# Sample attention of a hybrid decoder step: keys loaded by head pair, turned on VectorE in blocks of 32, scores of each sequence in four strips

## The reference, cut to what matters

```python
def dilated_attention_sample(q, k_all, v_all, rel_bias):   # q: (B=8, T=4, H=8, 64)
    for (w, d) in ((128, 1), (512, 4), (2048, 16)):        # keys at distance 0, d, 2d .. w
        ...
    s = einsum('bthc,btkhc->bthk', q, kg) * 64 ** -0.5 + bias
    p = softmax(where(valid, s, NEG))                      # one softmax over all key lists
    return einsum('bthk,btkhc->bthc', p, vg)
```

## Time and profile before

| | us |
|---|---|
| median of 3 runs | 1074.83 (1074.57 to 1074.99) |
| the profiled execution | 1073.11 |
| its span, first to last instruction | 1071.3 |
| start to the convolution stage | 281.2 |
| convolution stage with sample attention | 218.5 |
| output projection and router | 164.9 |
| experts | 272.1 |
| gated tail | 134.6 |

### The profile page before, as it was taken

How to read it: one execution, slowest core, us unless ns; L and a number is a source line. 1 busy time by engine, 2 the same in 40 slices (tenths; PEclk the granted TensorE clock), 3 DMA queues, 4 the chain that set the end, 5 groups by cost and what they waited for, 6 DMA issues and landing times.

```text
span 1071.3 us, 15537 instructions
## 1 busy us (share of the span) xinstructions
PE 1025.6 (96%) x5818; PEld 615.3 (57%) x5818; DVE 528.3 (49%) x1213; ACT 295.2 (28%) x621; POOL 177.6 (17%) x191
## 2 busy tenths in 40 slices
PE   6999999899999999999999998999999988899997
PEld 5888876556778877766445554334433323345443
DVE  4836545777753544344447875341111101068674
ACT  2332322777422321201002232111111111245331
POOL 0000000123600020015301223223131211130000
PEclk9999999899999999999999999999999989999999
DMA  9724133870654454656537534999999999784321
GB/s 320 193 86 147 44 92 107 231 212 20 219 167 155 148 163 152 219 204 230 213 118 294 203 127 161 405 403 420 418 414 414 421 413 398 311 342 165 123 79 79
DMA packets 103388, 241.85 MB, mean 226 GB/s; under 512 B 20342, under 2 KB 61214, under 8 KB 88784
## 3 DMA queue, kind: packets, MB, share of 16 engines
q1 hardware_dynamic: 92672, 211.83, 54.5%
q0 software_dynamic: 9920, 26.38, 6.4%
q10 hardware_dynamic: 720, 2.62, 0.6%
HBM read 206.84 MB, written 38.67 MB: 229 GB/s over the span
## 4 chain that ended last, share of the span: by engine, by line
PE 87%; DMA 7%; DVE 3%; issue 1%; ACT 1%; SPq 1%; POOL 0%; DVEq 0%; POOLq 0%; ACTq 0%
PE pair L2988 14%; PE pair L2678 13%; PE pair L3231 11%; PE pair L3338 7%; PE pair L3253 6%; PE pair L3076 5%; PE pair L3056 5%; DMA R<-in_w_down 3%; PE pair L3333 3%; PE pair L2812 2%; PE pair L2786 2%; PE pair L2827 2%; DMA R<-in_w_up 2%; PE pair L3218 2%; PE pair L2889 1%; PE pair L2906 1%
## 5 line engine op out<-in xcount | busy, mean ns | idle before, releaser
L2988 PE MATMUL pair<-R 128*128 128x264 f32 x672 | 160.4, 389 | 0.0
L3231 PE MATMUL pair<-R 128*32 128x512 f32 (+2 forms) x896 | 150.3, 603 | 6.4 <-DMA R<-in_w_up 4.8
L2678 PE MATMUL pair<-R 128*128 128x256 f32 x672 | 150.8, 384 | 2.4 <-DVE R L1730 2.4
L2678 PEld LDWEIGHTS pair<-R 128*128 128x128 f32 x672 | 128.0, 193 | 21.2 <-DVE R L1730 3.0
L2988 PEld LDWEIGHTS pair<-R 128*128 128x128 f32 x672 | 123.5, 190 | 23.0 <-issue 4.4
L2400 DVE TENSOR_TENSOR R<-pair,R 128x256 f32<-128x256 f32 x21 | 8.9, 425 | 208.7 <-ACT R L1542 208.7
L3231 PEld LDWEIGHTS pair<-R 128*32 128x32 f32 (+2 forms) x896 | 48.8, 125 | 92.4 <-issue 88.8
L3253 PE MATMUL pair<-R,bias 128*32 128x512 f32 (+2 forms) x448 | 79.0, 621 | 4.0 <-DMA R<-in_w_down 3.5
L3338 PE MATMUL pair<-R 128*128 128x512 f32 x168 | 73.0, 593 | 0.0
L3076 PE MATMUL pair<-R 128*128 128x512 f32 x128 | 58.5, 599 | 0.0
L3338 PEld LDWEIGHTS pair<-R 128*128 128x128 f32 x168 | 31.5, 190 | 38.2 <-issue 38.0
(11 more groups left out here) (383 smaller groups left out, 1496.5 us busy)
## 6 DMA issues: line engine op xcount, KB each, us to landing
R<-in_w_gate SPq DMA_DIRECT2D x32, 1024.0 KB, 15.6
R<-in_w_up SPq DMA_DIRECT2D x32, 1024.0 KB, 19.8
R<-in_w_down SPq DMA_DIRECT2D x32, 1024.0 KB, 21.0
R<-in_cache_k SPq DMA_DIRECT2D x8, 1024.0 KB, 5.1
R<-in_cache_v SPq DMA_DIRECT2D x8, 1024.0 KB, 4.9
R<-y_dram SPq DMA_DIRECT2D x16, 512.0 KB, 4.9
R<-in_w_in SPq DMA_DIRECT2D x15, 512.0 KB, 6.8
R<-xq_dram SPq DMA_DIRECT2D x1, 7168.0 KB, 26.1
```

The costliest lines, as they stand in the source:

```text
L2678: last = mm(qbank(p, part, k), lhs[:, c, :], rhs[:, c, :], start=(c == 0), stop=(c == 3))
L2988: last = mm(cbank(u, chain), w[:, c, :], xq[:, x, c, j, :], start=(c == 0 and n in (0, 1, 3)), stop=(c == 3), skip_group_check=True)
L3231: last = mm(bk[2 + u][r, :].rearrange("p (w f) -> p w f", w=2), xgT[u][:, c, r], wgu[s][:, :, c, :], start=(c == 0), stop=(c == DC - 1))
```

## The change

Keys are loaded otherwise. Per sequence and head pair `gg` one DMA brings the near rows and three bring the far rows, 128 features of 512 bytes each, to the 32 partitions `32*gg` and up: 16 DMAs to a key item where there were 4. On each partition lie 28 blocks of 128 features, one for each 32 keys. Values come with rows in another order, four DMAs as before, near rows as 2 KB pieces, far rows with the four rows of a group as the outermost dimension of the source.

VectorE turns the keys: `dve.transpose` of a 128 x 896 view, each 32 x 32 block by itself, four times per sequence, the j-th of every fourth feature. TensorE's 224 key turns and the copies behind them are gone. The contraction of a score now runs over 32 features of all four head pairs at once, four accumulating steps to a sequence, with a query tile that is zero outside its head. The four PSUM strips hold four quarters of the keys (256 columns each; the last one 128 cached keys and 4 x 32 columns for the new ones), so each sequence has its own 128 x 256 score tile, in two banks in turn. Every strip has its own minimum and sum; the exponentials are turned (2 turns per sequence) and weigh the values unnormalised; after sequences 3 and 7 the minima and sums are turned, a factor per strip is formed on VectorE and ACT, turned back and applied when the weighed values are masked. The bias table is made in strips too. The query and key of the sample tile are turned with every fourth column.

```diff
+        def load_item(i): ...
+            if kind == "k":
+                for gg in range(NG):
+                    rows, f = slice(32 * gg, 32 * gg + 32), slice(P * gg, P * gg + P)
+                    sp.dma_start(KL[i % 3][rows, 0:16, :], src[b][PAST - NEAR:PAST, f].rearrange("(k c) f -> c k f", c=32)).then_inc(arrived, 16)
+                    for k in range(FARC):
+                        sp.dma_start(KL[i % 3][rows, 16 + 4 * k:20 + 4 * k, :],
+                                     src[b][512 * k:512 * k + 512, f].rearrange("(c a) f -> c a f", a=16)[:, 0:4, :]).then_inc(arrived, 16)
+                return
+            sp.dma_start(near_kv, src[b][PAST - NEAR:PAST, :].rearrange("(s p) d -> p s d", s=4)).then_inc(arrived, 16)
             for k in range(FARC):
-                sp.dma_start(far_kv[:, k, :], src[b][512 * k:512 * k + 512, :].rearrange("(p a) d -> p a d", a=16)[:, 0:NT, :]).then_inc(S(f"ring_in{i % 3}"), 16)
+                sp.dma_start(far_kv[:, k, :], src[b][512 * k:512 * k + 512, :].rearrange("(c a) d -> a c d", a=16)[0:4]).then_inc(arrived, 16)
...
+        def turn_keys(b, j):          # VectorE
+            if j == 0:
+                slot, arrived = item("k", b)
+                dve.wait_ge(S(f"ring_in{slot}"), arrived)
+                if b >= 1:
+                    dve.wait_ge(S("ss_done"), b)
+            dve.transpose(keysT[:, j, :].rearrange("p (b n) -> p b n", n=32),
+                          KL[item("k", b)[0]][:, :, j:P:4]).then_inc(S("kt_done"), 1)
+
+        def score_sample(b): ...
+            dve.tensor_tensor_reduce(Es[b % 2], bk[6 + b % 2][:, 0:ROW], bias_s, -1.0, 3e38, ALU.add, ALU.min,
+                                     nms[:, b:b + 1]).then_inc(S("ss_scored"), 1)
...
         for u in range(UNITS):        # VectorE
...
             join_first(u)
-            if u >= 1:
-                sample_part(*SAMPLE_PARTS[k])
-            second_keys(*SAMPLE_PARTS[k])
+            if u == 1:
+                score_sample(0)
+            if 1 <= u < NB:
+                turn_keys(u, 0)
+                turn_keys(u, 1)
...
+            if 1 <= u < NB:
+                turn_keys(u, 2)
+                turn_keys(u, 3)
...
             join_lower(u)
...
             lower_out(u)
...
+            if 1 <= u < NB:
+                score_sample(u)
...
+            if u == 0:
+                spread_q(1)
             if u == 1:
+                spread_q(2)
...
+        def score_keys(b):            # TensorE
+            pe.wait_ge(S("kt_done"), 4 * b + 4)
...
+            for j in range(4):
+                start, stop = j == 0, j == 3
                 for k in range(FARC):
+                    mm(out[strips[k], 0:ROW].rearrange("p (h n) -> p h n", h=2), query(b)[:, j, :], keys_of[j][k], start=start, stop=stop)
+                mm(out[strips[3], 0:P], query(b)[:, j, :], keysT[:, j, FARC * P:NEAR], start=start, stop=False)
+                last = mm(out[strips[3], P:ROW].rearrange("p (a n) -> p a n", n=SAMP), query(b)[:, j, :],
+                          kts[:, j, :].unsqueeze(1).broadcast_to([P, 4, SAMP]), start=False, stop=stop)
...
             for n in range(PRODUCTS): # TensorE
                 conv_product(u, n)
...
+                if n == 1:
+                    if u == 1:
+                        score_keys(0)
+                    if 2 <= u <= NB:
+                        turn_ps(u - 1)
...
+                    if 5 <= u <= 9:
+                        sum_values(u - 5)
+                    if u >= 9:
+                        weigh_values(u - 4)
+                if n == 3 and u == 1:
+                    turn_ps(0)
+                if n == 3 and 4 <= u <= 8:
+                    weigh_values(u - 4)
+                if n == 5:
+                    if 1 <= u < NB:
+                        score_keys(u)
```

More of the change, by code:

```diff
@@ L64 @@
 SK = NEAR + FAR
-SKN = SK + SAMP
+ROW = 2 * P
+KEYS = SK
+KB = KEYS // 32
 CAP = 128
@@ L181 @@
 ITEMS = [("k", b) for b in range(5)] + [("v", 0), ("k", 5), ("v", 1), ("k", 6), ("v", 2), ("k", 7)] + [("v", b) for b in range(3, NB)]
+ISSUES = {"k": NG * (1 + FARC), "v": 1 + FARC}
 def item(kind, b):
     i = ITEMS.index((kind, b))
[L187 to L200, removed]
+    return i % 3, sum(16 * ISSUES[k] for k, _ in ITEMS[i % 3:i + 1:3])
+RING_USED = tuple(sum(16 * ISSUES[k] for k, _ in ITEMS[s::3]) for s in range(3))
 NSTAT = 6
@@ L480, in _build, with query @@
     PTf = view(R1, 20928, 2, 6, P)
[L482 to L486, removed]
+    keysT = view(R1, 14784, 4, KEYS)
+    keys_of = [[R1[:, 14784 + KEYS * j:14784 + KEYS * j + 1024].rearrange("p (h n) -> p h n", h=2)[:, :, P * k:P * k + P]
+                for k in range(FARC)] for j in range(4)]
+    Es = [view(R1, 18368 + ROW * k, ROW) for k in range(2)]
+    sx_min, sx_sum = (R1[0:4, 18880 + 32 * k:18912 + 32 * k] for k in range(2))
+    sx_d, sx_w = (R1[0:4, 18944 + P * k:18944 + P * k + P] for k in range(2))
+    PTs = view(R1, 19296, 4, 2, P)
+    qb = [view(bias, 512, 4, 4, 32), view(R1, 22368, 2, 4, 32), view(lg_all, 0, 2, 4, 32)]
+    def query(b):
+        return qb[0][:, b] if b < 4 else qb[b // 2 - 1][:, b % 2]
     sel = view(R1, 22624, NT)
+    head = misc[:, 3 * NE + 13:3 * NE + 15]
     as_raw = view(gqk, 0, CC, SAMP)
@@ L1435, in sample_part, with exp_sample @@
[L1435 to L1445 removed]
+        def exp_sample(b):
+            act.wait_ge(S("ss_scored"), b + 1)
+            act.activation(Es[b % 2], Es[b % 2], ACT.Exp, bias=nms[:, b:b + 1], scale=-1.0,
+                           accum_out=dens[:, b:b + 1]).then_inc(S("ss_exp"), 1)
@@ L2096, in normalise_sample, with spread_q @@
-        def normalise_sample(g):
-            dve.wait_ge(S("ss_exp"), g + 1)
-            then(dve.reciprocal(rdens, dens))
-            dve.tensor_scalar(Es, Es, rdens, None, ALU.mult).then_inc(S("ps_ready"), 1)
+        def spread_q(k):
+            first, n = ((0, 4), (4, 2), (6, 2))[k]
+            tok = slice(NT * first, NT * (first + n))
+            for gg in range(NG):
+                rows = slice(32 * gg, 32 * gg + 32)
+                for hh in range(2):
+                    dve.tensor_scalar(qb[k][rows, :, :, 8 * gg + hh:8 * gg + 8:2], qts[rows, :, tok].rearrange("p j (b t) -> p b j t", t=NT),
+                                      head[rows, hh:hh + 1], None, ALU.mult).then_inc(S("qbd"), 1)
@@ L2897, in score_keys @@
-        def score_keys(b):
-            g, bb = divmod(b, 4)
-            pe.wait_ge(S("kn_free"), 4 * b + 4)
-            pe.wait_ge(S("kf_free"), 4 * b + 4)
-            pe.wait_ge(S("qbd"), 8 * g + 8)
-            if bb == 0:
-                pe.wait_ge(S("ss_scored"), g) if g else pe.wait_ge(S("ot_free"), NGROUP)
-            for c0, c1, rhs in ((0, NEAR, near), (NEAR, SK, far), (SK, SKN, kts)):
-                for gg in range(NG):
-                    last = mm(bank[3][strips[gg], c0:c1], qbd[bb][:, gg, :], rhs[:, gg, :],
-                              start=(bb == 0 and c1 <= SK), stop=(bb == 3 and c1 != SK))
-            last.then_inc(S("ss_done"), 1)
@@ L2941, in sum_values @@
+            mm(bk[3][strips[3], :], PTs[:, b % 4, 1, 96:128], V[:, PT, :], start=False, stop=True).then_inc(S("so_full"), 1)
         def sum_values(b):
```

350 lines of the change are left out of this document (150 added, 200 removed).

## The result

The changed kernel took 1088.56 us (median of 4 runs, 1086.93 to 1090.78) against 1074.91 for the kernel before, timed beside it: ratio 1.0111, 95% interval 1.0085 to 1.0138. The forecast was 1060.8, faster. The profiled execution has a span of 1087.1 us where before had 1071.3.

The account below looks back on a forecast made before the run. TensorE was taken to bound the convolution stage: 194.1 us without waits plus 11.1 lost gives 205.2, 13.3 less; with the bias table 14.05 less, so 1059.1 profiled and 1060.8 median, range 1056 to 1064.

Parts of the forecast that it names:

- TensorE's work: Convolution stage without waits: 218.5 less 25.3 of key turns and 1.3 of wait, plus 1.4 scores and 0.8 turns, 194.1 us.
- The turn: VectorE's four 128 x 896 key turns per sequence: 1.09 us each, 4.3 per sequence, hidden from units 2 and 3 on.
- The keys' rate: Key loads at the stage's start: 512-byte pieces at 267 GB/s, 3.9 us per MB, SP's issue at 0.64 us slower.
- rival A: SP issues at 0.46 us per DMA, so weights land at 309 before they are wanted; 1051.9 us, chance 25%.
- the 11.1: Losses in first units: 1.0, 0.5, 4.3 for weights, 0.8, 1.2, 2.2 for turns and 1.1 for clock, 11.1 us.
- the forecast hole: Start of unit 2: TensorE stands still 3 to 6 us, ending when the weights land; a sign the forecast is right.
- The sum's term for the clock: First units, TensorE working about half the time: one clock fall of 3.4 us, 2.3 under the turns' wait, 1.1 counted.
- From unit 3 on the ring is ahead by 2 to 12 us: Loads from unit 3 on: data come 2 to 12 us ahead of need, so no loss was counted there.
- the 205.2 of the forecast: Whole convolution stage: 194.1 without waits plus 11.1 of losses, 205.2 us, 13.3 less than before.
- rival B: Values' far rows on four of sixteen DMA engines in units 4 to 7: about 4 us lost, 1064.8 us, chance 20%.
- Outside the stage: Later stages: order of events fixed relative to the convolution stage's end, so an earlier stage moves them as a whole.
- C: Keys into 32 partitions at half of 267 GB/s, 21 to 24 us lost, about 1073 us, no change; chance 10%.

Follow-up runs that it names:

- e7: Changed kernel with far values loaded with 32 as outermost dimension and weights of units 2 and 3 issued behind the first key item; 1061.19 us.
- e2: Changed kernel with VectorE turning 32 neighbouring features instead of every fourth; 1083.89 us, ratio to before 1.0030 to 1.0075.
- e1: Changed kernel with the far rows of the values loaded with 32 as the source's outermost dimension, as before; 1067.61 us, ratio 0.9884.
- e5: Kernel before with the far rows of the values loaded with four as the source's outermost dimension; 1089.90 us, ratio 1.0052 to 1.0151.
- e4: Changed kernel with values 32 outermost, scores reading keys in matching order, neighbouring features turned, weights of units 2 and 3 behind first key item; 1069.37 us.

## Why the prediction was wrong, step by step

- **TensorE's work: right.** It said 194.1 us for the stage without waits; e7 shows TensorE busy for 194.97 at full clock. A score takes 1.88 us, as worked out.
- **The turn: the wrong value within its bounds.** 1.09 was taken, 1.758 measured. The estimate fits a plain read (1070 ns in e2), but the kernel reads one of every four fp32. The row with just that step had given a factor of 1.6 an element and so 1.6 us; measured is 1.64 times the plain turn as a whole. The nearest row was set aside for a price that leaves out the step. The price of the slower turn: 6.5 us of waits, of which e2 gives back 1.6 in the stage.
- **The keys' rate: too fast, and the first waits near by luck.** 267 GB/s was read from weights that go to 128 partitions; pieces for 32 partitions ran at 183. SP was quicker than said (0.48 us an issue instead of 0.64, as rival A had it), so for most of the way the data set the pace and not the issue. The two errors nearly cancel: the weights came 37.1 us after the start of the stage, where 36.6 was said. The terms behind the 11.1 did not come true all the same. Keys 0 were not late: VectorE turned them from 299.1 on, without a wait for a load. But the four turns took 6.75 us instead of 4.3, so TensorE waited 3.25 for the scores of sequence 0 and 3.25 for those of sequence 2, where 1.0 and 2.2 were said, and none at the weights, where 4.3 was said: it came to unit 2 after they had landed. VectorE did stand for them, 3.2 us, and the chain of waits runs from them through the turns to the scores of sequence 2. e2, with the turn that was forecast, has the forecast hole, 3.2 us. That e1, without late values, has a stage of 208.2, 14.1 above 194.1 where 11.1 was said, is therefore no proof of the sum: 8.7 of the 14.1 are standstill, the rest is clock. The sum's term for the clock, one fall of 3.4 us of which 1.1 counts, was an estimate, and no run shows the 1.1. Before, the clock stood at 0.50 for 6.8 us after a stretch with TensorE busy for 3.7 of 5.6 us; in the changed kernel it stood there for 6.8 us from 304.7 on, in e1 for 3.4 us from 304.0 and 6.8 from 334.7, and in e2 for 3.4 us from 319.0.
- **"From unit 3 on the ring is ahead by 2 to 12 us": the step that failed.** TensorE waited 4.5 us for the values of sequence 1, 2.2 for those of sequence 2, 9.7 for sequence 3 and 0.7 later, 17.1 in all, and its clock fell to 0.50 twice there. The stage was 21.0 us longer than the 205.2 of the forecast, and e1 gives back 18.0 of them; the other 3.0 are the first waits and the clock. The mechanism stood in the text as rival B with 20%, and with the right rate (98 GB/s on four engines; 101 at a share of 0.26, 4.2 of 16, in e5) and the right place, the values of sequence 3. Its price of 4 was too small: it reckoned 6.9 us for the keys of a unit, and at 183 GB/s the 1.83 MB take 10.0. With that its own sum reads 10.7 + 10.0 + 1.9 = 22.6 us per unit of 17.7, four times 4.9 less 3 of lead: 16.6. This is near the 17.1, but it was worked out afterwards, and e5, where keys are fast and the loss is 13.5, shows that it is not the whole account. How much the slow keys add to the late values stays open, since no run had quick keys and values by four in the changed kernel.
- **Outside the stage: not in the sum.** Of the 27.8 us between 1060.8 and 1088.56 some 7 lie in front of the stage and behind it, where the forecast moved all events as a whole; their cause stays open.
- **The chances.** Each rival was priced alone. B came true, and C in part (183 instead of 267 GB/s, not half), and both lengthen the same stream of loads; no case held both.

## What to carry to other kernels

Look at the outermost dimension of a DMA's source before its bytes: here a reordering that put a 4 there cost three quarters of the rate (101 GB/s where 32 gave 382) and held SP behind it (issues of 5 us where they took 0.6), and free engine time did not cover it. Before a shorter stage is put down to a wait that has gone, compare standstill and busy time: in e7 the standstill was the same and the clock was not. Price an instruction by the row with its reading step, not by the row with its size. When a mend makes another engine read in steps, as in e4, look at that engine's instruction times first; the gain may be spent there.

## What the runs showed of the hardware

- Far rows of 2 KB: 101 GB/s at a share of 0.26 with four as the outermost dimension, 182 at 0.57 with eight, 382 at 1.05 with 32. By four, four pieces are in flight, and each takes 84 ns as before. A far load gives 5, 9 and 16 rises of its semaphore.
- A 128 x 896 fp32 turn in blocks of 32 on VectorE: 1070 ns from neighbouring elements, 1758 from every fourth.
- A record of a matmul of 32 weight columns and 256 moving fp32 columns (the trace has two to each matmul of the program): 382 ns, and 634 with the moving operand in steps of 32.
- Pieces of 512 bytes: 183 GB/s into 32 partitions at a time, 50 to 56 ns each; 229 into 128, 27 to 30 ns each, at a share of 0.81.
